# Diffusion backbone on eight cores: two thirds of layer 0's adaLN modulation moved into the attention loop, and Fourier matmuls issued in groups

## The reference

```python
def adaln(cvec, w_mod, b_mod):
    m = jax.nn.silu(cvec) @ w_mod + b_mod        # w_mod: 1024 x 6144 in each layer
    return m.reshape(cvec.shape[0], 6, D_MODEL)

for l in range(DEPTH):                            # DEPTH = 2
    m_lat = adaln(c, w_mod[l], b_mod[l])
    m_ctx = adaln(c_ctx[None], w_mod[l], b_mod[l])
    hc = modulate(rmsnorm(cx, norm1[l]), m_ctx[:, 0], m_ctx[:, 1])
    hl = modulate(rmsnorm(lat, norm1[l]), m_lat[:, 0], m_lat[:, 1])
    zl = hl @ w_in[l]
    lat = lat + m_lat[:, 2][:, None, :] * token_mixers(zl, kl, vl, *mixer_params, rope, (kc, vc))
    hf = modulate(rmsnorm(lat, norm2[l]), m_lat[:, 3], m_lat[:, 4])
    lat = lat + m_lat[:, 5][:, None, :] * conv_ffn(hf, w_up[l], w_conv_ffn[l], w_down[l])
    # the context stream the same way, in layer 0 only
```

## Time and profile before

| | |
|---|---|
| median of 3 runs | 4102.01 us |
| lowest | 4101.84 us |
| profiled execution: its time | 4098.53 us |
| its span, slowest core (core 1) | 4097.0 us |
| spans of the eight cores | 4076.4 to 4097.0 us |
| TensorE, VectorE, ScalarE, GpSimd busy | 79%, 48%, 36%, 12% of the span |
| granted TensorE clock, mean of a core | 0.894 to 0.899 |

### The profile page before, as it was taken

The page is one execution under the profiler, slowest core; times in us unless marked ns, Lnnn a source line. Parts: engine busy times, 40 slices in busy tenths (PEclk is TensorE's granted clock), DMA queues, the critical chain, the costliest instruction groups (busy, mean ns, idle before and its releaser), DMA issues.

```text
span 4097.0 us, 51278 instructions; the slowest of 8 cores (4076.4 to 4097.0 us)
## 1 busy us (share of the span) xinstructions
PE 3251.0 (79%) x15660; PEld 1382.9 (34%) x15660; DVE 1978.9 (48%) x2539; ACT 1487.5 (36%) x2622; POOL 476.0 (12%) x518
## 2 busy tenths in 40 slices
PE   2479587878888887887777686899988887888885
PEld 2135222222444433433332233222233332333332
DVE  0502511111556568777777405111136667777775
ACT  2313466656111123222223314777721113222224
POOL 0000200000233220000000001000023331000000
PEclk7599888989999988999998898999989997999996
DMA  8361111110111131111110341000011112211102
GB/s 191 55 163 41 47 24 36 27 32 10 32 33 21 29 54 25 26 26 26 26 17 0 79 127 39 1 1 1 1 33 33 33 33 42 36 31 32 31 6 82
DMA packets 56708, 162.14 MB, mean 40 GB/s; under 512 B 5888, under 2 KB 6912, under 8 KB 54912
## 3 DMA queue, kind: packets, MB, share of 16 engines
q0 software_dynamic: 26784, 95.56, 13.3%
q1 hardware_dynamic: 29664, 63.31, 5.1%
HBM read 246.02 MB, written 8.39 MB: 62 GB/s over the span
## 4 chain that ended last, share of the span: by engine, by line
PE 60%; DVE 15%; DMA 11%; issue 6%; ACT 5%; POOL 2%; DVEq 0%; ACTq 0%; POOLq 0%; SPq 0%
PE ps L457 60%; DMA ring<-wbr 3%; DVE Vt L479 3%; DMA mreg<-dftl 3%; DMA ring<-wmod 3%; DVE tf L479 2%; DVE KTt L479 2%; ACT pbuf L467 2%; DVE tf L476 2%; DVE hT L472 1%; ACT tb L467 1%; DMA big<-x 1%; DVE latT L479 1%; POOL rs L476 1%; POOL tf L476 1%
## 5 line engine op out<-in xcount | busy, mean ns | idle before, releaser
L457 PE MATMUL ps<-hT,ring 128*128 128x512 bf16 (+1 forms) x6416 | 1428.0, 379 | 108.9 <-DMA ring<-win 58.2
L457 PEld LDWEIGHTS ps<-hT,ring 128*128 128x128 bf16 x6416 | 641.5, 101 | 828.4 <-issue 177.1
L467 ACT ACTIVATE mreg<-ps 128x512 bf16<-128x512 f32 (+1 forms) x1168 | 626.5, 592 | 231.8 <-PE ps L457 231.0
L479 DVE SCALAR_TENSOR_TENSOR latT<-ps,vecs,latT 128x512 f32<-128x512 f32 x896 | 623.9, 745 | 55.8 <-PE ps L457 22.6
L457 PE MATMUL ps<-mreg,Vt 128*128 128x512 bf16 (+1 forms) x1168 | 473.4, 405 | 66.5 <-ACT mreg L467 66.4
L457 PE MATMUL ps<-big 128*128 128x512 bf16 (+1 forms) x1584 | 353.2, 387 | 191.1 <-DVE big L476 189.5
L467 ACT ACTIVATE tb<-ps 128x512 bf16<-128x512 f32 (+1 forms) x334 | 191.3, 573 | 807.8 <-PE ps L457 796.2
L457 PE MATMUL ps<-mreg,cbt 128*128 128x512 bf16 (+1 forms) x1168 | 468.7, 401 | 0.0
L467 ACT ACTIVATE pbuf<-ps 128x512 bf16<-128x512 f32 (+1 forms) x396 | 203.5, 589 | 644.8 <-PE ps L457 531.3
L476 POOL TENSOR_TENSOR rs<-rs,tf 128x512 f32<-128x512 f32 (+1 forms) x180 | 216.6, 1203 | 1388.1 <-DVE tf L863 771.3
L457 PEld LDWEIGHTS ps<-big 128*128 128x128 bf16 x1584 | 161.1, 103 | 383.7 <-issue 225.8
(11 more groups left out here) (74 smaller groups left out, 2223.4 us busy)
## 6 DMA issues: line engine op xcount, KB each, us to landing
mreg<-dftl SPq DMA_DIRECT2D x128, 256.0 KB, 2.9
ring<-wmod POOLq DMA_DIRECT2D x48, 512.0 KB, 7.8
ring<-win POOLq DMA_DIRECT2D x48, 512.0 KB, 7.0
ring<-wup POOLq DMA_DIRECT2D x44, 512.0 KB, 5.3
big<-wdn POOLq DMA_DIRECT2D x12, 1024.0 KB, 8.4
mreg<-rope SPq DMA_DIRECT2D x40, 256.0 KB, 2.7
big<-x SPq DMA_DIRECT2D x4, 2048.0 KB, 13.5
out<-big SPq DMA_DIRECT2D x4, 2048.0 KB, 6.6
```

What stands on the lines that cost most here:

```text
L457: ins = e.matmul(out, l, r, start=(first and i == 0), stop=(last and i == n - 1))
L467: return P.op("act", lambda e, out=out, in_=in_, func=func, kw=kw: e.activation(out=out, in_=in_, func=func, **kw), reads, writes)
L479: return P.op(eng, lambda e: e.scalar_tensor_tensor(out, in0, scalar, in1, op0, op1), reads, writes)
```

## The change

Three things. Only blocks 0 to 7 of layer 0 stay at the start; the other 16 go to the head of `pending_mod`, ahead of layer 1's 24, and the loop takes a block after every seventh pair instead of every tenth. `layer_vecs` is cut in two: what the first norm needs at the layer's start, the rest after attention. And the matmuls of a Fourier step, before two operations with a semaphore update each, are one operation (`fnx`, `fny`).

```diff
-        for blk in range(24):
+        for blk in range(8):
             mod_block(0, blk)
-        pending_mod = [(l_, blk) for l_ in range(1, DEPTH) for blk in range(24)]
+        pending_mod = [(0, blk) for blk in range(8, 24)] + [(l_, blk) for l_ in range(1, DEPTH) for blk in range(24)]
...
-        def layer_vecs(l):
+        def layer_vecs(l, part):
+            if part == 0:
+                dma("pool", bdpm[:, :, :].rearrange("p a b -> p (a b)"), bdpm_d[:, l * 256:(l + 1) * 256], (), (buf("bdpm"),))
+                for s in range(2):
+                    o_n = _off["norm1"][0] + l * 8
+                    stt("dve", vecs[:, s, 0, :], modT[:, l, 8:16, s], 1.0, smalls[:, o_n:o_n + 8], ALU.add, ALU.mult,
+                        (mod_b, sm_b), (vec_b,))
+                    P.op("dve", lambda e, s=s: e.tensor_copy(vecs[:, s, 1, :], modT[:, l, 0:8, s]), (mod_b,), (vec_b,))
+                return
+            for s in range(2):
...
-            layer_vecs(l)
+            layer_vecs(l, 0)
...
+                        def fnx(e, bk=bk, ti=ti):
+                            ins = None
+                            for k in range(2):
+                                ins = e.matmul(bk[:, k * 256:(k + 1) * 256], big[:, 6 + k, ti * 128:(ti + 1) * 128], bdcs,
+                                               start=True, stop=True)
+                            return ins
+                        P.op("pe", fnx, (bigb(6, c0t), bigb(7, c0t), cb_b), (bkb,))
...
-                            for k in range(2):
-                                mm(bks[k][0][:, 0:W],
-                                   [(xcs_all[:, ti, k, 0, :], d3[:, 0, 0:W]), (xcs_all[:, ti, k, 1, :], d3[:, 1, 0:W])],
-                                   (BG(ti * 512, ti * 512 + 512), dsb), (bks[k][1],), first=(i == 0), last=(i == ntl - 1))
+                            def fny(e, bks=bks, ti=ti, d3=d3, W=W, i=i, ntl=ntl):
+                                ins = None
+                                for k in range(2):
+                                    for cs in range(2):
+                                        ins = e.matmul(bks[k][0][:, 0:W], xcs_all[:, ti, k, cs, :], d3[:, cs, 0:W],
+                                                       start=(i == 0 and cs == 0), stop=(i == ntl - 1 and cs == 1))
+                                return ins
+                            P.op("pe", fny, (BG(ti * 512, ti * 512 + 512), dsb), (bks[0][1], bks[1][1]))
...
-                    if pending_mod and pi % 10 == 9:
+                    if pending_mod and pi % 7 == 6:
                         l_m, blk_m = pending_mod.pop(0)
                         mod_block(l_m, blk_m, SP[pi % 2][0])
...
+                layer_vecs(l, 1)
```

More of the change, by code:

```diff
@@ L543, in build_nc @@
         idb_ap = cbs(CB_ID)
-        def layer_vecs(l):
+        def layer_vecs(l, part):
[8 more added lines that the diff above has]
+            for s in range(2):
+                P.op("dve", lambda e, s=s: e.tensor_copy(vecs[:, s, 2, :], modT[:, l, 16:24, s]), (mod_b,), (vec_b,))
+                o_n = _off["norm2"][0] + l * 8
+                stt("dve", vecs[:, s, 3, :], modT[:, l, 32:40, s], 1.0, smalls[:, o_n:o_n + 8], ALU.add, ALU.mult,
+                    (mod_b, sm_b), (vec_b,))
+                P.op("dve", lambda e, s=s: e.tensor_copy(vecs[:, s, 4, :], modT[:, l, 24:32, s]), (mod_b,), (vec_b,))
+                P.op("dve", lambda e, s=s: e.tensor_copy(vecs[:, s, 5, :], modT[:, l, 40:48, s]), (mod_b,), (vec_b,))
+            return
             for s in range(2):
@@ L693, in layer @@
                         bk, bkb = bka()
-                        for k in range(2):
-                            mm(bk[:, k * 256:(k + 1) * 256], [(big[:, 6 + k, ti * 128:(ti + 1) * 128], bdcs)],
-                               (bigb(6 + k, c0t), cb_b), (bkb,))
+                        def fnx(e, bk=bk, ti=ti):
[5 more added lines that the diff above has]
+                        P.op("pe", fnx, (bigb(6, c0t), bigb(7, c0t), cb_b), (bkb,))
                         act(xcs_all[:, ti, :, :, :].rearrange("p k s c -> p (k s c)"), bk[:, 0:512], AF.Identity,
```

## The result

| | kernel before | changed kernel |
|---|---|---|
| median, 42 runs each | 4104.85 us | 4121.67 us |
| lowest | 4097.57 us | 4112.9 us |
| ratio to the kernel before | | 1.0029 (95%: 1.0015 to 1.0042) |

What follows compares the result with a forecast made beforehand. Loads bound the start; in attention, blocks early in a chunk wait for loads queued behind the previous chunk's cast. -49.6 - 1 + 71 = +21 us on the 4102 us median gave 4123 us, range 4085 to 4150.

Steps and rivals of the forecast that it cites:

- The sign: Whole kernel: +21 us, called no change within 2% (chance 0.93), leaning slow.
- The start: Layer 0's start: with sixteen blocks gone, the first norm follows block 8 instead of block 24, 49.6 us saved.
- Attention: Layer 0's attention: sixteen more blocks at new places, 34 us own cost plus 37 us stalls, 71 us longer.
- The price by place: Attention chunks: first block costs 10.8 us at p = 0, falling about 1.5 a pair; a block with load ready 2.1.
- Vector scalings: Layer starts: eight of twelve small vector ops go behind attention; up to 2.2 us to win at layer 1, 1 taken.
- Fourier grouping: Fourier steps: same matmuls with merged semaphore updates and waits, cost 0, bounds 13 us either way.
- (a): Attention: an added block costs only its own 2.1 us whatever its place, a gain, 4085 us; chance 0.10.
- (b): Attention: a chunk's three loads delay each other, +25 us and perhaps another 10 to 15, 4160 us; chance 0.12.
- (c): Attention: with three blocks a chunk TensorE's clock stays low, 66 us on top, 4190 us; chance 0.04.
- (d): Attention and Fourier stage: blocks hidden as in (a) and all Fourier load waits lost, below 4020 us; chance 0.02.
- (e): Layer 0's start: something else holds the first norm, only part of the 50 us returns, some 4150 us; chance 0.02.
- The waits forecast in words: TensorE in attention: `wmod` waits up from 10 to about 15 and 37 to some 65 us; vector-op waits 40, about 33.

Runs made afterwards that it cites:

- after_again: The changed kernel submitted once more with no edit: median 4114.25 us, ratio 1.0040 to the kernel before.
- start_only: Kernel before with layer 0's modulation blocks 8 to 23 left out, a constant in their place and nothing added to attention: 4050.32 us, ratio 0.9873.
- fourier_only: Kernel before with only the Fourier matmuls grouped, one operation and semaphore update for each step: ratio 1.0001.
- before_early_loads: Kernel before with each attention block's load issued two blocks ahead, its 24 blocks still at every tenth pair: 4046.22 us, ratio 0.9849.
- early_loads: Changed kernel with each attention block's load issued two blocks ahead, matmul places unchanged: 4023.68 us, ratio 0.9810 to the kernel before.
- late_places: Changed kernel with blocks after pairs 9, 12 and 15 of each latent chunk, loads where they were in the queue: 4024.5 us, ratio 0.9799.
- early_places: Changed kernel with blocks after pairs 1, 8 and 15 of each latent chunk, none in context chunks: 4143.31 us, ratio 1.0091 to the kernel before.
- edge_places: norm_blocks with layer 1's 24 blocks after pairs 1 and 17 of twelve latent chunks: ratio 0.9806, profiled execution 4024.88 us.
- norm_blocks: Changed kernel with layer 0's 16 blocks in the first norm phase, layer 1's 24 at every tenth pair, loads two blocks ahead: ratio 0.9757, profiled 4005.34 us.
- mid_places: norm_blocks with layer 1's 24 blocks after pairs 6 and 12 of twelve latent chunks: ratio 0.9741, profiled execution 4005.84 us.
- places_9_17: norm_blocks with layer 1's 24 blocks after pairs 9 and 17 of twelve latent chunks: ratio interval 0.9488 to 1.0063, profiled execution 4025.75 us.

## Why the prediction was right

4123 us was forecast, 4121.67 measured. That the two medians meet so closely is luck: the ratio says +12 us (6 to 17) where the sum said +21, and the median of 42 stands 7 us above that of after_again. The sign, "no change" and the mechanism are right; each of the two large terms is within 6 us of what was measured, and a gain of 4 us in layer 1 was not in the sum. Its terms:

**The start, -49.6 us.** Right. On core 1 the last block's matmuls begin at 79.66 us instead of 130.66, 51 earlier; start_only gives 52 us (46 to 59) for this alone. In the changed kernel some of it is gone before attention: the first context chunk's copy is 43.6 us earlier on core 1 and 45.2 on the mean of six cores. The Fourier stage, which nothing should have touched, took 97.2 us there instead of 94.3 on core 1; but start_only, whose Fourier code is that of before, takes 97.2 on core 1 too, and fourier_only 97.4 without being slower as a whole. In all three the longest matmul of the stage is 631 to 634 ns, where it is 379 in the profile of before: a stretch at the lower clock that some executions have. What is missing from the 50 is a difference between executions: before_early_loads, whose code up to attention is that of before, ends its third context chunk 4.5 us later than the profile of before in the mean of the eight cores (498.2 against 493.7 us), and against it the changed kernel (448.8) is 49.4 us earlier.

**Attention, +71 us.** Measured on core 1: 570.0 - 512.95 = 57.1 for the latent chunks and 12.87 - 3.92 = 8.95 for the context one, 66 us; the mean of the eight cores gives 65.5. The price by place held for each type of chunk within 3 us (over 26.9):

| blocks after pairs | forecast | measured |
|---|---|---|
| 0, 7, 14 | 15.0 | 13.9, 13.4 |
| 1, 8, 15 | 13.5 | 14.6, 12.9 |
| 2, 9, 16 | 12.1 | 11.3, 10.4 |
| 3, 10, 17 | 8.5 | 10.3, 10.0 |
| 4, 11 | 7.0 | 6.9, 6.9 |
| 5, 12 | 5.3 | 2.5, 5.3, 5.2 |
| 6, 13 | 4.2 | 3.7, 2.5 |
| 1 | 9.3 | 9.8 |
| context | 8 | 8.95 |

The reason given, that the loads stand behind the previous chunk's cast in GpSimd's queue, is shown by early_loads and late_places, which take the stall away from either side and land together, and by early_places, which adds to it (half of what the price list promised).

**How the 71 was split** is the part that was off. I had put 34 us on the blocks' own cost (2.1 each) and 37 on stalls. The own cost is 1.25 us (early_loads; late_places gives 48.2 / 40 = 1.2), so the sixteen more account for 20 and the stalls, with the clock behind them, for the rest. The 2.1 came from a chunk with one block at p = 9 at a mean clock of 0.88 against bare chunks at 0.94: part of it was the clock. In before_early_loads the same chunk takes 28.16 us at a mean of 0.94, 1.26 over a bare one. Since I priced whole chunks, the total stood; but the expectation for early_loads, made with 2.1, promised 65 us and it gave 91.

**Vector scalings, -1 us.** At layer 1's start the first norm op comes 1.37 us after the first scaling (2257.22 to 2258.59) instead of 3.37: 2.0 us, near the upper bound. Behind attention the scalings lie under the wait for `win` (12.38 us, was 12.60), as forecast:

```profile
1049.25 1.87 PE L457 MATMUL ps<-hT,ring 128*128 128x256 bf16 x8 [12.38 <-DMA ring<-win]
```

**Fourier grouping, 0.** Right. (The "86 us" of the prediction is the stretch of the earlier trace rows, 236 to 322 us; the whole stage is the 94.3 us above.)

**What is left.** At layer 1's start core 1 is 21.9 us late and at the end 15. Over the eight cores layer 1 is 4.3 us shorter in the mean, but from 10.7 shorter to 2.9 longer; 2 of it are the scalings. The only other edit that touches layer 1 is the Fourier grouping, and fourier_only is 0.1 us away from before there in the mean, yet up to 8 us on single cores. So the rest may be no more than the difference between executions; I leave it open. With the spread of the slowest core it is why +21 at the end of attention became +12 to +15 at the end.

**The rivals.** (a), that place does not matter, is out for this kernel. With early loads place still counts, but much less: chunks with three blocks take 29.1 to 32.5 us there, where they took 36.9 to 41.5. (b), three loads slowing each other: the first of three took 6.6 us from issue to TensorE's start in chunk 1, but 5.3 and 5.4 in chunks 8 and 10, as the 5.4 of the earlier trace rows and of chunk 15, which has one load alone; no steady cost. The estimate of 3.2 us by the Trainium skill, page "DMA: Bandwidth & Descriptors", section "Anatomy of one DMA — SWDGE (gpsimd) path", weighed in the prediction, would have been short here as well. (c), the clock: three blocks a chunk don't hold it down, the chunks' means are 0.83 to 0.91 and low where the stalls are long, and the clock does cost (18 us of TensorE's busy time in attention, by early_loads); but edge_places shows that a block in a bad place can cost its chunk some 3 us that way. (d) and (e) did not come about.

The waits forecast in words: "about 15" and "some 65 us" for `wmod`, measured 14 and 81.6; 40 and 33 us for the vector op, measured 40 and 32.1.

## What to carry to other kernels

A wait in a trace is not the whole price of a stall: 37 us of waits were worth 61, since the clock was lower behind them. Work that is spread through a loop "where the engine has time" carries its loads with it, and a load goes when its queue gets there, not when the data could be had. Before moving such work, look at what stands ahead of its load in the issuing queue; issuing two blocks ahead was worth 62 us in the kernel before and 91 in the changed one, when the move itself was worth -12. And look for a phase in which the transfer engines are idle: sixteen blocks in the first norm phase cost 10 to 14 us there, where they cost 52 at the start, and that version (norm_blocks, or mid_places with its 24 blocks in the middle of the chunks) is the fastest of all, 2.4% and 2.6% under the kernel before.

## What the runs showed of the hardware that I had not expected

An attention chunk has two lengths for the same work: 25.3 us at a mean granted clock of 1.00 and 26.9 at 0.94 when bare (25.33 and 26.83 are neighbours on core 1 of mid_places), 27.8 and 29.4 with two blocks in the middle. The clock falls for some 3 to 4 us behind the chunk's end, after TensorE has stood 2.0 us while the accumulators are copied, in some chunks and not in others of the same kernel (in mid_places the stop is 2.03 us in chunks of both kinds). With a further stop of 0.8 us just ahead of that one, from a block after pair 17, it fell in every chunk from the third to the twelfth of places_9_17, on all eight cores, and made them 30.4 to 30.9 us long; in edge_places, with the same pair of stops, single chunks escaped.
